# A two-block transformer kernel on one core: last scatter, norm and split handed over block by block, query copies moved, row sums as single-pass products

## The reference, cut to what matters

```python
def reference(x, ...):
    x = first_block(x, ...)        # layer 0: mixer + swiglu; layer 1: mixer + moe_swiglu
    return second_block(x, mem_2, ...)

def moe_swiglu(xn, ...):           # top 2 of 8 experts
    for e in range(N_EXPERTS):
        out = out + combine[:, e:e + 1] * swiglu(xf, w_gate_up[e], w_down[e])

def hybrid_layer(x, mem, ...):
    hn = rmsnorm(x, pre_g)
    proj = hn @ w_in               # 6664 columns, in pieces: xbc, z, dt, mem_q, sb_q, ret_q, ...
    y_ssd = ssd_mixer(xbc, z, dt_raw, ...)
    y_mem = memory_read(mem_q, mem_n, w_mem_kv)     # k, v = split(rmsnorm(mem) @ w_mem_kv)
    ...

def ssd_mixer(...):
    da = (delta * -exp(a_log)).reshape(b, nc, L, SSD_HEADS)
    a_cs = cumsum(da, axis=2)
    seg = a_cs[:, :, :, None, :] - a_cs[:, :, None, :, :]
    decay_in = exp(where(causal, seg, -inf))        # the rows of seg need a_cs along the free axis
```

## Time and profile before

| | |
|---|---|
| median of 3 runs | 2156.13 us (2155.09 to 2156.83) |
| profiled execution, its time | 2158.86 us |
| profiled execution, its span | 2157.1 us |
| PE busy | 2128.0 us, 99% of the span |
| DVE, ACT busy | 1594.5 us (74%), 1335.9 us (62%) |
| mean granted PE clock | 0.998 |

### The profile page before, as it was taken

One profiled execution on the slowest core, in us unless ns is written; L12 is line 12 of the kernel. 1 busy time (PEld: TensorE's weight loads), 2 busy tenths in 40 slices (PEclk: granted clock), 3 DMA queues, 4 the chain that ended last, 5 costly groups with the idle time before them and its releaser, 6 DMA issues.

```text
span 2157.1 us, 27820 instructions
## 1 busy us (share of the span) xinstructions
PE 2128.0 (99%) x10919; PEld 1804.9 (84%) x10919; DVE 1594.5 (74%) x1349; ACT 1335.9 (62%) x1160; POOL 78.7 (4%) x68
## 2 busy tenths in 40 slices
PE   7999999999999999999999999999999999999998
PEld 6978888888788888888888888888878898898987
DVE  5577555466767888888888888888897667565665
ACT  5465544355657777776777777777675555455553
POOL 3100000000000000000000000000110000000000
PEclk9999999999999999999999999999999999999999
DMA  8554665554557999999999999999996534455442
GB/s 283 158 180 163 211 199 185 172 197 149 195 176 278 390 386 381 374 388 367 388 380 376 374 377 382 372 382 374 387 384 239 176 118 156 165 177 172 137 156 79
DMA packets 249454, 570.74 MB, mean 265 GB/s; under 512 B 12201, under 2 KB 14385, under 8 KB 249105
## 3 DMA queue, kind: packets, MB, share of 16 engines
q1 hardware_dynamic: 242368, 546.41, 70.6%
q0 software_dynamic: 5280, 17.22, 2.4%
q10 hardware_dynamic: 1712, 5.83, 0.7%
HBM read 563.12 MB, written 6.30 MB: 264 GB/s over the span
## 4 chain that ended last, share of the span: by engine, by line
PE 92%; DMA 3%; DVE 3%; ACT 1%; issue 1%; SPq 0%; DVEq 0%; ACTq 0%
PE bank L929 36%; PE bank L1193 9%; PE bank L1194 9%; PE bank L1197 9%; PE bank L935 9%; PE bank L1241 4%; PE bank L1234 4%; PE bank L1236 4%; PE bank L976 3%; DMA ring<-w_in 1%; DMA ring<-moe_w_down 1%; DVE halves_r L2268 1%; ACT w_high L1970 1%; DVE w_low L2716 0%; PE bank L1355 0%
## 5 line engine op out<-in xcount | busy, mean ns | idle before, releaser
L2716 DVE TENSOR_TENSOR w_low<-ring,w_high 128x4096 fp32r<-128x4096 f32 x167 | 736.5, 4421 | 80.3 <-ACT w_high L1970 79.1
L1970 ACT ACTIVATE w_high<-ring 128x4096 fp32r<-128x4096 f32 x167 | 607.2, 3636 | 233.4 <-DMA ring<-moe_w_gate_up 141.2
L929 PE MATMUL bank<-halves_r,xT_high 128*128 128x512 f32 (+1 forms) x1856 | 561.9, 381 | 4.7 <-ACT halves_r L1730 3.2
L2268 DVE TENSOR_TENSOR halves_r<-ring,halves_r 128x2048 fp32r<-128x2048 f32 x174 | 389.1, 2264 | 150.7 <-ACT halves_r L1730 148.7
L929 PEld LDWEIGHTS bank<-halves_r,xT_high 128*128 128x128 f32 x1856 | 343.4, 188 | 71.4 <-issue 5.6
L1730 ACT ACTIVATE halves_r<-ring 128x2048 fp32r<-128x2048 f32 x175 | 326.3, 1892 | 117.3 <-DMA ring<-w_in 55.0
L1193 PE MATMUL bank<-w_high,xg_high 128*128 128x512 f32 x896 | 354.6, 396 | 0.0
L1194 PE MATMUL bank<-w_high,xg_low 128*128 128x512 f32 x896 | 349.5, 390 | 0.0
L929 PE MATMUL bank<-halves_r,xT_low 128*128 128x512 f32 (+1 forms) x928 | 348.3, 379 | 0.0
L1197 PE MATMUL bank<-w_low,xg_high 128*128 128x512 f32 x896 | 221.6, 389 | 0.0
L929 PEld LDWEIGHTS bank<-halves_r,xT_low 128*128 128x128 f32 x928 | 175.3, 189 | 31.7
(11 more groups left out here) (400 smaller groups left out, 2297.1 us busy)
## 6 DMA issues: line engine op xcount, KB each, us to landing
ring<-moe_w_gate_up SPq DMA_DIRECT2D x224, 1024.0 KB, 10.6
ring<-moe_w_down SPq DMA_DIRECT2D x112, 1024.0 KB, 9.8
ring<-w_in SPq DMA_DIRECT2D x108, 1024.0 KB, 5.1
ring<-w_out SPq DMA_DIRECT2D x24, 1024.0 KB, 4.9
ring<-ffn_w_gate_up SPq DMA_DIRECT2D x22, 1024.0 KB, 5.2
ring<-ffn_w_down SPq DMA_DIRECT2D x11, 1024.0 KB, 4.9
ring<-w_mem_kv SPq DMA_DIRECT2D x8, 1024.0 KB, 5.1
ring<-w_branch_attn SPq DMA_DIRECT2D x4, 1024.0 KB, 5.0
```

The costliest lines, as they stand in the source:

```text
L929: return pe.matmul(o[:, a:a + n], x[:, c, b * P:(b + 1) * P], w[:, k, col:col + n], **flags)
L1970: act.activation(high_slot(k), ring[:, ring_r.slot(names[k]), :], ACT.Copy).then_inc(w_high_in[r], 1)
L2268: dve.tensor_tensor(raw_view(half, halves_r), raw_view(half), top_view(half).bitcast(F32), ALU.subtract).then_inc(raw_low_in, 1)
L2716: dve.tensor_tensor(w_low[:, slot, :], ring[:, slot, :], high_slot(k).bitcast(F32), ALU.subtract).then_inc(w_low_in[r], 1)
```

## The change

1. In the handover, h is given over in two steps: `h_new` goes up after block 0 and again after block 1 (counts of all later waits on `h_new` are one higher). ACT norms block 0 on the first. The memset of `tmpd` goes away.
2. On DVE the order becomes: norm of block 0, half of the low of MV half 1 (two of its four chunks), norm of block 1, the other half, the four `xT_low` pieces, the lows of both X0 halves, then two new small instructions for point 4, then the copy of parameters. On ACT the top of X0's half 1 goes behind the four `xT_high` pieces.
3. The copies of MQ0 and MQ1 stand ahead of the wait for `dt_abs` on ACT, in both layers.
4. The row sums take fp32r operands. The order of the constants becomes ident, lt, ge, flip, le, ones; in layer 0 `flip` is set to zero and the 384 columns (zero, `le`, `ones`) are rounded in place to `sums_r`. `da` is split into `da_high` and `da_low` on DVE (two new instructions of 16 columns in each layer). For each head there are four products of 256 columns: high and low part, each with (`le`, `ones`) for block 0 and (zero, `le`) for block 1.

```diff
-            scattered(("SCL",))
-            link(dve.memset(tmpd, 0.0))
-            dve.sem_inc(h_new, 1)
-            split(("MV", 0), (1,))
+            for b in range(TB):
+                scattered_block(("SCL",), b)
+                dve.wait_ge(*drained(("SCL", b, 1)))
+                dve.sem_inc(h_new, 1)
...
-                link(dve.tensor_copy(par[:, 16:80], par_all[:, l, 16:80]))
...
-                for b in range(TB):
-                    norm(b, 8 + 2 * l + b + 1, pre_rows[l])
-                split(("X0", l))
+                if l == 0:
+                    half = (("MV", 0), 1)
+                    rest, whole, top = raw_view(half, halves_r), raw_view(half), top_view(half).bitcast(F32)
+                    norm(0, 9, pre_rows[0])
+                    dve.wait_ge(top_in, split_at[half] + 1)
+                    dve.tensor_tensor(rest[:, 0:2, :], whole[:, 0:2, :], top[:, 0:2, :], ALU.subtract)
+                    norm(1, 10, pre_rows[0])
+                    dve.tensor_tensor(rest[:, 2:4, :], whole[:, 2:4, :], top[:, 2:4, :],
+                                      ALU.subtract).then_inc(raw_low_in, 1)
+                else:
+                    for b in range(TB):
+                        norm(b, 10 + b + 1, pre_rows[1])
+                    split(("X0", l))
...
+                if l == 0:
+                    split(("X0", l))
+                    link(dve.memset(flip, 0.0))
+                    link(dve.tensor_copy(sums_r[:, :], flat(consts[:, 3:6, :])))
+                link(dve.tensor_copy(par[:, 16:80], par_all[:, l, 16:80]))
...
-                    norm(b, (h_new, l + 1))
+                    norm(b, (h_new, b + 1 if l == 0 else 3))
-                split(("X0", l))
+                split(("X0", l), (0,) if l == 0 else None)
...
+                if l == 0:
+                    split(("X0", l), (1,))
...
+                copy2(qmT[:, 0:2, :], "MQ0")
+                copy2(qmT[:, 2:4, :], "MQ1")
                 act.wait_ge(dt_abs, l + 1)
...
-                        pe.matmul(o[:, a:a + P], da(0).to_broadcast([P, P]), le, start=True, stop=True)
-                        pe.matmul(o[:, a + P:a + SEQ], da(0).to_broadcast([P, P]), ones, start=True, stop=False)
-                        mm = pe.matmul(o[:, a + P:a + SEQ], da(1).to_broadcast([P, P]), le, start=False, stop=True)
+                        for part in (da_high, da_low):
+                            for b in range(TB):
+                                da = part[:, 8 * b + 2 * k + j:8 * b + 2 * k + j + 1].to_broadcast([P, P])
+                                mm = pe.matmul(o[:, a:a + SEQ], da, sums_r[:, P - b * P:P - b * P + SEQ],
+                                               start=part is da_high and b == 0, stop=part is da_low and b == 1)
...
-                ins.then_inc(da_ready, 1)
+                link(ins)
+                link(dve.tensor_copy(da_high[:, :], s2[:, 48:64]))
+                dve.tensor_tensor(da_low[:, :], s2[:, 48:64], da_high[:, :].bitcast(F32), ALU.subtract).then_inc(da_ready, 1)
```

More of the change, by code:

```diff
@@ L67, in common_constants @@
     t, s = i[:, None], i[None, :]
-    parts = [t == s, t + s == P - 1, t <= s, t < s, t >= s, np.ones((P, P)), np.broadcast_to(s, (P, P))]
+    parts = [t == s, t < s, t >= s, t + s == P - 1, t <= s, np.ones((P, P)), np.broadcast_to(s, (P, P))]
     return np.concatenate([np.asarray(x, np.float32) for x in parts], axis=1)
@@ L424, in kernel_program @@
         sb("half_line", [P, P // 2])
-        consts = sb("consts", [P, 7, P])
-        ident, flip, le, lt, ge, ones, slots_row = (consts[:, k, :] for k in range(7))
+        consts, consts_at = placed("consts", [P, 7, P])
+        ident, lt, ge, flip, le, ones, slots_row = (consts[:, k, :] for k in range(7))
+        sums_r = rounded("sums_r", [3 * P], consts_at + 4 * 3 * P)
+        le_kept, ones_kept = sums_r[:, P:2 * P].bitcast(F32), sums_r[:, 2 * P:3 * P].bitcast(F32)
         ARENA = 25344
@@ L617, in kernel_program @@
         tmpd = C(TB, P)
+        da_high = rounded("da_high", [TB * 8], arena_at + 4 * (C.at + 192))
+        da_low = rounded("da_low", [TB * 8], arena_at + 4 * (C.at + 208))
         small2 = C(256)
@@ L886, in _ @@
             for k, (b, a, z) in enumerate(pieces):
-                sp.wait_ge(h_new, LAYERS + 1 + k)
+                sp.wait_ge(h_new, LAYERS + 2 + k)
                 sp.dma_start(t["out"][0, b * P:(b + 1) * P, a:z], h[:, b, a:z]).then_inc(x1_in_out_done, 16)
@@ L1390, in ssd_row_sums @@
                     for j in range(2):
-                        da = lambda b: small2[:, 48 + 8 * b + 2 * k + j:49 + 8 * b + 2 * k + j]
                         a = j * SEQ
-                        pe.matmul(o[:, a:a + P], da(0).to_broadcast([P, P]), le, start=True, stop=True)
-                        pe.matmul(o[:, a + P:a + SEQ], da(0).to_broadcast([P, P]), ones, start=True, stop=False)
-                        mm = pe.matmul(o[:, a + P:a + SEQ], da(1).to_broadcast([P, P]), le, start=False, stop=True)
+                        for part in (da_high, da_low):
[3 more added lines that the diff above has]
+                                               start=part is da_high and b == 0, stop=part is da_low and b == 1)
                     mm.then_inc(*end(f"AR{k}", l))
@@ L1413, in stick_sums @@
                     pe.matmul(o[:, P:SEQ], ge, s[:, P:SEQ], start=True, stop=False)
-                    pe.matmul(o[:, P:SEQ], ones, s[:, SEQ:TRI], start=False, stop=True)
+                    pe.matmul(o[:, P:SEQ], ones_kept, s[:, SEQ:TRI], start=False, stop=True)
                     pe.matmul(o[:, SEQ:TRI], ge, s[:, SEQ:TRI], start=True, stop=True).then_inc(*end(f"TS{hd}", l))
@@ L1479, in _ @@
                 o = begin("AC", l)
-                pe.matmul(o[:, 0:8], le, da[:, 0:8], start=True, stop=True)
-                pe.matmul(o[:, 8:16], ones, da[:, 0:8], start=True, stop=False)
-                pe.matmul(o[:, 8:16], le, da[:, 8:16], start=False, stop=True).then_inc(*end("AC", l))
+                pe.matmul(o[:, 0:8], le_kept, da[:, 0:8], start=True, stop=True)
+                pe.matmul(o[:, 8:16], ones_kept, da[:, 0:8], start=True, stop=False)
+                pe.matmul(o[:, 8:16], le_kept, da[:, 8:16], start=False, stop=True).then_inc(*end("AC", l))
                 pe.wait_ge(*(drained("MK1", l - 1) if l else (maps_in, 32)))
@@ L1666, in _ @@
                 else:
-                    pool.wait_ge(h_new, 2)
+                    pool.wait_ge(h_new, 3)
                 pool.dma_start(post_row, t["post_norm_g_2"][l].partition_broadcast(P)).then_inc(rows_in, 16)
@@ L2147, in _ @@
                 act.activation(par[:, 80:88], par[:, 64:72], ACT.Exp).then_inc(par_exp, 1)
-                copy2(qmT[:, 0:2, :], "MQ0")
-                copy2(qmT[:, 2:4, :], "MQ1")
                 split(("SQ", l))
@@ L2694, in gathered, with scattered_block @@
                                       ALU.subtract).then_inc(*fr(job))
+            def scattered_block(tag, b, i=None):
+                for n in range(2):
+                    job = (*tag, b, n)
+                    dve.wait_ge(*full(job, i))
+                    v = h[:, b, n * WIDE:(n + 1) * WIDE]
+                    dve.scalar_tensor_tensor(out=v, in0=out_of(job)[:, :], scalar=rt[:, 167 + b:168 + b], in1=v,
+                                             op0=ALU.mult, op1=ALU.add).then_inc(*fr(job))
             def scattered(tag, i=None):
                 for b in range(TB):
[L2698 to L2703, removed]
+                    scattered_block(tag, b, i)
                 for b in range(TB):
```

## The result

The changed kernel takes 2144.41 us (median of 5 runs, 2144.1 to 2144.49) against 2155.77 us before (median of 5, 2155.09 to 2156.83): ratio 0.9947, 95% interval 0.9937 to 0.9958. It is 11.4 us faster; 10.9 were forecast, as 2145.0 us.

A forecast was written before the change was run, and what follows sets the result against it. The prediction took PE as the bound, busy 2128.0 of 2157.1 us. Its terms 6.6 + 1.3 + 3.0 = 10.9 us, from the median 2156.13, gave 2145.2, stated as 2145.0 us, range 2141 to 2149.5.

The forecast's parts named there:

- Reading of the bound: PE busy 2128.0 of 2157.1 us; from 1650 us its one long wait is 4.0 us for `xT_low`, then half clock.
- Part 1: Handover before X0: X0 starts at 1650.05 instead of 1654.58 and keeps full clock; worth 6.6 us.
- the clock's term: X0's first products after the handover: running at full instead of half clock gives 2.1 us.
- the clock stays at 1.00: At X0's start, PE's remaining gap of about 0.5 us leaves full clock, as over two gaps of 0.34 us.
- Part 2: Query copies earlier on ACT: PE's stop of 0.67 us before MG in each layer goes; worth 1.3 us.
- the bound of 1.7: Most the query copies can give before MG, if the preceding record's modelled tail (0.17 us each) is idle too.
- Part 3: Row sums on PE: eight fp32r products at 0.12 us replace six fp32 at 0.222, in 8 calls; worth 3.0 us.
- Sum: Whole kernel: 6.6 + 1.3 + 3.0 = 10.9 us less, forecast as 2145.0 us.
- (a): Rival at X0's start: clock falls anyway, 2.1 us lost, 2147.2 us; chance 0.10, together with DVE coming late.
- (b): Rival in the row sums: they save nothing, operand read or type switch costing the saving; 2148.0 us, chance 0.08.
- (d): Rival in the row sums: products run as full fp32, two records each, making it slower; 2166 us, chance 0.02.
- (c): Rival in the handover: the wait only moves to X0's low; the change gives 4.3 us or less; chance 0.05.

The follow-up runs named there:

- p3_sums: Only the row sums changed to fp32r products (point 4) on the kernel before; 2152.32 us, ratio 0.998.
- p2_queries: Only the copies of MQ0 and MQ1 moved ahead of the wait for `dt_abs`, on the kernel before; 2154.82 us, ratio 0.9992.
- p1_swap_only: Only DVE's lows of both X0 halves moved behind the `xT_low` pieces, on the kernel before; 2153.18 us, ratio 0.9984.
- a_one_signal: The changed kernel with h given over in one step again, after both blocks; 2145.95 us, ratio 0.9952 to the kernel before.
- a_sums_fp32: The changed kernel with row sums as two fp32 products of 256 columns a head, `da` unsplit; 2150.63 us, ratio 0.9975 to the kernel before.

## Why the prediction was right

**Reading of the bound.** Right. The 4.0 us entry, the half clock behind it and the two gaps ahead of MG were nearly all of PE's listed idle time from 1630 us on, and the parts alone nearly add up to the whole.

**Part 1.** Forecast 4.5 us of wait and 2.1 of clock, 6.6; measured 4.82 + 2.10 = 6.92 between the two profiles. `xT_low` came 0.3 us sooner than worked out: ACT had the first signal 2.15 us after the scatter's first product, not 2.3, and DVE's pieces followed each other a little closer. That the clock's term came out at 2.1 is in part luck: it was taken from one execution and measured against the same one, and two other kernels with the same wait lose 1.5 us. That the clock stays at 1.00 was taken from two gaps of 0.34 us. The second of them was misread: the profile has 0.34 us of idle time ahead of the transposes and 0.10 among them (0.27 us over the pace, by the starts). It did no harm, because the gap left ahead of X0 was smaller than the 0.5 us worked out: 0.25 us beyond the last product's own time.

**Part 2.** The cause was right, the size at the upper bound: 1.75 us (0.87 and 0.88) instead of 1.34. The tail of the record before the gap is idle too, as the bound of 1.7 had it.

**Part 3.** Forecast 3.0 us, measured 3.4 by p3_sums against p2_queries from AC on. A product costs 0.113 us (second call: 1728.62 to 1728.85 for two), not the 0.12 of X0's rows. The Trainium skill (page "TensorE: Matmul & The Clock Gate", section "Back-to-back issue gap") gave 109 ns for an isolated product at full clock, which I set aside for the row. The measured 113 lies nearer to it, and its 3.7 us for the row sums errs by 0.3, mine by 0.4.

**Sum.** All three terms were forecast too low, 10.9 us against 12.1 by the stretches (4.82 + 2.10 + 1.75 + 3.4). The medians show 11.4. A part of this difference can be that executions of the kernel before lose now 1.5 and now 2.1 us to the clock; that was not measured in the executions without a profile, so the closeness of 2145.0 to 2144.41 owes something to luck.

**The rivals.** (a), the clock falls anyway: it does not in the changed kernel, but p1_swap_only shows how near it is, and my expectation for that run was wrong on this point. Sixteen transposes with two short gaps beside them do not lower it: they stand in a_one_signal too, at 1.00. And transposes run at full clock. At the start of the program, where products of 512 columns are 0.43 us apart instead of 0.23 (the trace has no clock row there), eight transposes take about twice the time that they take in a_one_signal; before, then a_one_signal:

```profile
9.15 1.94 PE L976 MATMUL bank<-consts,xs 128*128 128x128 f32 x8 [9.15 <-DVE xs L2253]
```

```profile
1644.22 1.03 PE L980 MATMUL bank<-consts,xs 128*128 128x128 f32 x8
```

By this the rule in the Trainium skill, page "TensorE: Matmul & The Clock Gate", section "Part 4: PE-mode transpose", that the full clock does not engage for them, does not agree with the traces. Whether transposes by themselves would keep the clock for long, no run here shows. (b) fell with p3_sums (422.5 to 419.16 us from AC on), (d) by the one record a product; a_sums_fp32 measured the price of two (6.5 us, where the fp32 case of (d) needed four such products a head). (c): no wait took the old one's place.

## What to carry to other kernels

When the bound engine waits for the last of a helper's jobs, list what the helper did before and ask of each when its reader wants it; moving the late-wanted one and giving the input over in pieces each gave little alone (2.1 and 0.4 us) and 4.8 together. Price a wait of PE with the clock behind it. In these profiles waits up to 0.6 us cost only themselves, waits near 2 us cost 1.5 us more in three of four, and waits of 4.0 and 4.5 us cost 1.5 to 2.5 more each time. A product with a 0/1 operand can go as a high and a low single-pass product for half the fp32 price of the same shape (0.9 us a call against 1.7; against the narrower fp32 products of before, 1.33, a third was saved), as long as the engine that must split the other operand has the time: in the row sums it was 16 columns, in the stick-breaking sums 384, and there the gain became a wait.

## What the runs showed of the hardware that was not expected

- The granted clock can fall after the work has come back: in p1_swap_only PE had worked for 1.5 us at full clock behind a gap of 1.9 us when the clock went to 1.2 GHz, for 3.4 us; in its second profile, in p2_queries and in p3_sums it fell 0.4 to 0.6 us behind X0's first product.
- The same gap of 2.3 us in the same kernel kept the clock in one execution (48.41 us from X0 to DT) and lost it in another (49.89 us).
- Single-pass products of 128 columns are 0.06 us apart and of 384 columns 0.18 us, in a group of four; fp32 ones of 128 columns 0.22 us.
